# Small products of a doubling scheme, made per 64 tokens in quarters of the PE array

## What is computed

```
a_mat = where(strict, einsum('bhncd,bhnsd->bhncs', kb, k) * gamma, 0.0)
t_mat = a_mat + eye(C)
u = triangular_solve(t_mat, v * beta, lower, unit_diagonal)
w = triangular_solve(t_mat, kb * exp(gc), lower, unit_diagonal)
...
v_new = u_n - w_n @ S
o     = qd @ S + qk_n @ v_new
S     = S * gl + kd^T @ v_new
```

## Time and profile before

| | us |
|---|---|
| median of 3 runs (lowest to highest) | 4056.29 (4054.85 to 4060.84) |
| the profiled execution | 4052.51 |
| its span, first to last instruction | 4050.7 |
| mean granted TensorE clock | 0.993 of 2.4 GHz |
| the stage with the delta rule and the attention | 428.7 to 923.6, 494.9 long |
| PE busy in the span | 3928.2 |

### The profile page before, as it was taken

One profiled execution on the slowest core, in us unless ns is written; L12 is line 12 of the kernel. 1 busy time (PEld: TensorE's weight loads), 2 busy tenths in 40 slices (PEclk: granted clock), 3 DMA queues, 4 the chain that ended last, 5 costly groups with the idle time before them and its releaser, 6 DMA issues.

```text
span 4050.7 us, 47347 instructions
## 1 busy us (share of the span) xinstructions
PE 3928.2 (97%) x19500; PEld 3204.4 (79%) x19500; DVE 2166.8 (53%) x3208; ACT 1673.7 (41%) x2626; POOL 17.1 (0%) x34
## 2 busy tenths in 40 slices
PE   4999999998999999999999999999999999999999
PEld 2777899886788877887778878987778777778887
DVE  6541555554733465874657846345646446646333
ACT  3351556664433353444534335233335233334333
POOL 0000000000000000000000000000000000000000
PEclk9999999998999999999999999999999999999999
DMA  4112000003242222222222222222222222223232
GB/s 167 53 57 70 10 5 6 23 16 119 83 120 94 94 89 87 75 88 89 89 89 76 82 93 91 87 89 78 83 84 94 89 89 78 80 87 114 94 95 87
DMA packets 113869, 323.44 MB, mean 80 GB/s; under 512 B 26920, under 2 KB 34040, under 8 KB 113656
## 3 DMA queue, kind: packets, MB, share of 16 engines
q1 hardware_dynamic: 111416, 314.91, 24.3%
q0 software_dynamic: 2240, 5.51, 0.7%
HBM read 303.86 MB, written 18.06 MB: 79 GB/s over the span
## 4 chain that ended last, share of the span: by engine, by line
PE 92%; DVE 4%; ACT 2%; DMA 1%; issue 1%; SPq 0%; DVEq 0%; ACTq 0%
PE ps L311 49%; PE ps L289 25%; PE ps L1027 4%; PE ps L1022 2%; PE ps L1316 1%; PE ps L1033 1%; PE ps L1293 1%; PE ps L725 1%; PE ps L2412 1%; PE ps L1301 1%; PE ps L1852 1%; PE ps L421 1%; DVE a L508 0%; PE ps L1103 0%; PE ps L1341 0%
## 5 line engine op out<-in xcount | busy, mean ns | idle before, releaser
L311 PE MATMUL ps<-a,w_hi 128*128 128x512 f32 (+1 forms) x6128 | 1875.2, 391 | 14.9 <-DVE a L508 6.7
L311 PEld LDWEIGHTS ps<-a,w_hi 128*128 128x128 f32 x6128 | 1126.3, 189 | 287.3 <-issue 27.5
L311 PE MATMUL ps<-a,w_lo 128*128 128x512 f32 (+1 forms) x3064 | 1163.4, 386 | 0.0
L262 DVE TENSOR_TENSOR w_lo<-w_raw,w_hi 128x1024 fp32r<-128x1024 f32 x539 | 658.1, 1221 | 447.1 <-ACT w_hi L257 444.1
L257 ACT ACTIVATE w_hi<-w_raw 128x1024 fp32r<-128x1024 f32 x539 | 564.1, 1051 | 564.4 <-DMA w_raw<-in_w_mlp 346.5
L311 PEld LDWEIGHTS ps<-a,w_lo 128*128 128x128 f32 x3064 | 571.3, 189 | 122.9
L289 PE MATMUL ps<-h_hi,w_hi 128*128 128x512 f32 x1536 | 490.0, 401 | 1.9 <-DVE xT L361 1.9
L289 PE MATMUL ps<-h_hi,w_lo 128*128 128x512 f32 x1536 | 481.6, 395 | 0.0
L289 PE MATMUL ps<-h_lo,w_hi 128*128 128x512 f32 x1536 | 481.5, 395 | 0.0
L356 DVE TENSOR_TENSOR h_lo<-u_sq,h_hi 128x512 fp32r<-128x512 f32 x192 | 132.9, 692 | 491.3 <-ACT h_hi L346 491.3
L361 DVE TENSOR_TENSOR xT<-xT,ps 128x1024 f32<-128x1024 f32 x192 | 234.1, 1220 | 289.9 <-PE ps L289 289.1
(11 more groups left out here) (358 smaller groups left out, 3328.4 us busy)
## 6 DMA issues: line engine op xcount, KB each, us to landing
w_raw<-in_w_mlp SPq DMA_DIRECT2D x384, 512.0 KB, 3.4
w_raw<-in_w_in SPq DMA_DIRECT2D x107, 512.0 KB, 3.5
w_raw<-in_w_out SPq DMA_DIRECT2D x48, 512.0 KB, 3.5
xT<-in_x SPq DMA_DIRECT2D x2, 2048.0 KB, 11.6
x<-xT SPq DMA_DIRECT2D x2, 2048.0 KB, 7.6
xT<-x SPq DMA_DIRECT2D x2, 2048.0 KB, 12.7
rpb_rows<-in_rpb SPq DMA_DIRECT2D x1, 3810.0 KB
z<-staged SPq DMA_DIRECT2D x4, 512.0 KB, 3.8
```

Of the source, the lines that this page charges most:

```text
L262: nc.vector.tensor_tensor(w_lo[u.z][:, :], w_raw[u.z][:, :], w_hi[u.z][:, :].bitcast(F32), ALU.subtract).then_inc(w_split[u.z], 1)
L311: last = nc.tensor.matmul(ps[:, bank, 0:t1 - t0], w[:, k * P:(k + 1) * P], a[:, h, low, k, t0:t1], start=(i_k == 0 and i == 0), stop=(i_k ...
```

## The change

Up to level 5 each product of `half_heads` becomes two: tokens 0 to 63 with tokens 0 to 63, and 64 to 127 with 64 to 127. Each takes 64 rows and 64 columns of the array (a quarter of it, the two on its diagonal) and 32 moving columns in place of 64, and writes to 64 partitions of the same bank. The blocks off the diagonal are no longer written; the mask of the level is 0 there, and DVE's L1208 reads the bank in whole as before. The subtraction (L1215) is made for the two quarters apart, so that it reads only what was written; the semaphore is raised by the second. Level 6 is as it was.

```diff
+        def quarters(l):
+            if l == NL - 1:
+                return [(slice(0, P), slice(0, 1))]
+            n = GRID >> l + 1
+            return [(slice(GRID * i, GRID * i + GRID), slice(n * i, n * i + n)) for i in range(2)]
...
             def half_heads(b, lhsT, rhs, l, which):
                 for h in range(GH):
-                    last = nc.tensor.matmul(halves(pbank(b), l, which)[:, h], lhsT[:, h, :], halves(rhs[:, :, :], l, which)[:, h],
-                                            start=True, stop=True)
+                    for side, pairs in quarters(l):
+                        last = nc.tensor.matmul(halves(pbank(b), l, which)[side, h, pairs], lhsT[side, h, side],
+                                                halves(rhs[:, :, :], l, which)[side, h, pairs], start=True, stop=True)
                 return last
...
                         dve.wait_ge(gs["X"], upper(n, d, l))
                         dve.wait_ge(gs["Dt"], level(n, d, l - 1))
-                        part = halves(g_Dt[d][:, :, :], l, 1 - d)
-                        nc.vector.tensor_tensor(part, part, halves(pbank(cross_bank(d, l)), l, 1 - d), ALU.subtract).then_inc(gs["Dt"], 1)
+                        for side, pairs in quarters(l):
+                            part = halves(g_Dt[d][:, :, :], l, 1 - d)[side, :, pairs]
+                            ins = nc.vector.tensor_tensor(part, part, halves(pbank(cross_bank(d, l)), l, 1 - d)[side, :, pairs], ALU.subtract)
+                        ins.then_inc(gs["Dt"], 1)
```

## The result

The changed kernel takes 4028.16 us (median of 6 runs, 4025.7 to 4030.75), the kernel before beside it 4056.26 (4054.85 to 4061.45). The ratio is 0.9928, 95% interval 0.9917 to 0.9939: 28 us less, where 29 were forecast. The profiled execution took 4026.77 us with a span of 4025.0, 25.7 less than before.

A forecast was written before the change was run, and what follows sets the result against it. PE's order of work was taken to bound the stage; 80 blocks saving 39.2 us, less 3.7 and 5.9 held back by ACT, gave -29.6 us, 4027 us as median. The range was 4007 to 4079, the forecast's own 4007 to 4038.

The forecast's parts named there:

- The bound: Stage of the edited function, 428.7 to 923.6 us: PE never runs dry and its order of work sets the length.
- A couple's price: Two quarter records, one per row half, in a changed block: 0.062 us a couple, 16 couples 0.99 us.
- The estimate of 0.100 a couple: Changed blocks: if a 25 ns start-to-start floor held for loads too, 0.100 us a couple, +10 us, 4066.
- do two row groups run together?: Changed blocks on PE: yes, from L2412's 64-row operands; a couple costs what one full-array record costs, 0.111 us.
- The change of form: PE going between full array and quarters: 0.30 us for entering and leaving a block, ends 0.25 and 0.40.
- What ACT doesn't let through: PE's L1301 waiting for ACT's copies: 0.73 us lost in each of 5 chunks, 3.7 us.
- The last three chunks: PE already waits for ACT there: the saving of four blocks a chunk counted as lost, 5.9 us.
- One of the prediction's low cases: Changed blocks at 0.062 us, form changes 0.40, same ACT loss: 0.39 a block, 31 - 8 = 23 us, 4033.
- Same bank: Rival: both quarters write one PSUM bank and run one behind the other, +40 us, 4096; chance 0.12.
- Issue: Rival: PE's instruction stream sets the pace, so a couple stays at 0.111 us, +24 us, 4080; chance 0.13.
- Gain eaten: Rival: PE waits at g_D, g_gu or g_Dt, or couples take 0.070 to 0.086; at most half stays, 4038 to 4048; chance 0.12.
- DVE's split: Subtraction L1215 in two: 15 us more of DVE, covered by PE's other work, costing nothing; uncovered, at most 8 us.

The follow-up runs named there:

- e3: Changed kernel, but each product takes all 128 rows and 64 columns of the array, still 32 moving columns: 4025.2 us, ratio 0.9912.
- e2: Changed kernel, but quarters for direction 0 only, in products and subtraction, direction 1 as before: 4053.0 us, ratio 0.9985.
- e6: Changed kernel with the first two of the attention's four copies a row made by DVE in place of ACT: 4019.7 us, ratio 0.9903.
- e8: Kernel before, with every product of levels 1 to 6 made in two column halves, all 128 rows and 64 moving columns, one subtraction: 4018.8 us, ratio 0.9902.
- e10: The changed kernel measured once more, nothing altered: 4025.2 us, ratio 0.9911.
- e9: Kernel before, with all products of levels 1 to 6 in column halves and two attention copies a row on DVE: 4008.9 us, ratio 0.9866.
- e1: Changed kernel, but all four heads of tokens 0 to 63 come ahead of those of tokens 64 to 127: 4049.0 us, ratio 0.9976.
- e7: Changed kernel, but levels 1 to 4 in four pieces of 32 tokens, with four subtractions in place of two: 4026.5 us, ratio 0.9921.
- e4b: Changed kernel with each of DVE's two subtractions made in two again, two heads each: 4030.9 us, ratio 0.9930.

## Why the prediction was right

**The bound.** PE's order of work set the stage's length, as the earlier trace rows had been read: up to chunk 4 what the blocks save comes off the chunk but for one new wait.

**A couple's price** was mis-sized by little: 0.062 us forecast, 0.058 measured. Its way there was right (loads set the pace, columns count, rows don't). The estimate of 0.100 a couple, named there among the rivals, is out with it. But "do two row groups run together?" was the question for the wrong dimension: e3 shows that the rows are not needed.

**The change of form:** 0.30 forecast, 0.34 by e2 and e6. A block saves 0.54 us (e6's early chunks, 5.40/10), where 0.49 were in the sum: 43 us for 80 blocks in place of 39.

**What ACT doesn't let through** in chunks 0 to 4 was 3.7 us in the sum. The first quarter product starts at 430.1 us and its chunk ends 45.4 later; before it was 428.9 and 49.7, so chunk 0 saved 4.3. With chunks 1 to 4 of the table that is 22.2 of 5 x 5.4 = 27.0: 4.8 us lost. e6 shows the cause, for the 0.95 us a chunk come back when the two copies leave ACT.

**The last three chunks** were the step that was mis-sized: 5.9 us forecast, 16.2 - 6.1 = 10.1 measured. The prediction counted ACT there and named a fall of the clock only among the things that would make it wrong. PE's waits grew from 4.5 us to 11.3. The clock is the rest: before, one window of the three was below 1.00 (0.97 of 65.3 us); in the changed kernel 0.97 of 65.4 and 0.92 of 64.7 us. The second of these stands against e8, whose last chunk has the same waits (2.1 us n_pt, 1.4 g_D, 1.1 g_vt, as here) and no fall:

```profile
825.90:885.50 59.60, 54.30 (x695) 47.72 (x694) 32.47 (x98) 45.83 (x98) 0.00 (x0) 1.00 0.14 37
```

59.6 us against 64.7. Some 0.8 us of the 5.1 belong to the level 6 that e8 shortens (57.82 - 57.05 = 0.77 in early chunks), about 4 to the clock; half of 10.2 us at half speed is 5.1. Other traces agree. The table adds up, by the granted clock of each trace, how long it stood at 0.50 while PE had work; the last chunk mark is the product with g_R that ends the chunk table above:

| | last three chunks, us | of it at 0.50 | last chunk mark to the end, us | of it at 0.50 | that less half of the column before |
|---|---|---|---|---|---|
| before | 196.5 | 3.4 | 3126.3 | 34.1 | 3109.3 |
| changed | 190.4 | 13.7 | 3127.7 | 37.5 | 3108.9 |
| e10, changed again | 192.8 | 20.5 | 3124.4 | 30.7 | 3109.1 |
| e3 | 188.6 | 10.2 | 3127.8 | 37.5 | 3109.0 |
| e6 | 182.9 | 10.2 | 3132.3 | 47.8 | 3108.4 |
| e8 | 182.6 | 3.4 | 3129.1 | 41.0 | 3108.6 |
| e9 | 177.2 | 3.4 | 3134.8 | 47.8 | 3110.9 |

e3's chunks are as long as the changed kernel's where both have the full clock. Between e3 and e10 the last three differ by 4.2 us for 10.3 us more at 0.50. The changed kernel has 10.3 us more at 0.50 than the kernel before, so an estimate from these rows is that 4.2 of the 10.1 us are the clock's, and 5.9 are left for ACT, which is what the prediction had counted for it. So what failed in this term is that it had nothing for the clock. What decides when the clock falls no run shows: waits of PE aren't needed for it (e1).

These two errors, +4 us on the blocks and -5 on what is held back, cancel. The stage is 28.3 us shorter; 1.2 were lost ahead of it (its first product comes at 430.1 in place of 428.9) and 1.4 behind it, so the two profiled executions are 25.7 apart, where the sum had 29.6. That the sum met the time so closely is luck, and so is the median that it met, since the second measurement gave 36 us; that it lay within the range is not. One of the prediction's low cases is mis-added: it speaks of the same loss to ACT and takes 8 us where the sum has 9.6, which would make it 4035 in place of 4033.

**The rivals.** *Same bank* is out: 32 loads in 1.01 us, two row groups into one bank. The Trainium skill, TensorEngine Tiling (Array Packing), Gotcha 1: PSUM Pressure, says that different row tiles can't access a bank simultaneously; with different partitions in that bank, the 1.01 us disagree, and the measurement decides. Whether it holds for the same partitions no run tried. *Issue* is out: e7 sends out 64 loads and 64 matmuls in about 0.65 us. *Gain eaten* took a third of it, 15 of 43 us, less than the half that I had given that case.

**DVE's split** cost nothing, as forecast, and e4b doubled it for nothing.

**After the stage** 1.4 us of the 27.1 by which the last chunk mark comes earlier are given back. Of e6's 12.9 us against the changed kernel at that mark its span shows 8.3, of e9's 23.2 it shows 16.1. The table's last columns say where these go. The work behind the mark is the same in all, and what differs is how long the clock stood at 0.50: less half of that time, it is 3108.4 to 3109.3 us in six of the seven. e9's 2 us more are one wait, for n_z, of 13.0 us in place of 10.8. Why those later falls come where they do is open.

## What to carry to other kernels

Where a small product is bound by its weight loads, split its output in halves of the array's columns and issue the halves in turn: loads of half the width then run side by side, with nothing left out of the product and no rows to give up. Keep such products together, since entering and leaving them costs about 0.34 us, and alternate the parts. Then look at what the freed PE runs into: here another engine's copies, and a clock that fell more often among the short blocks, with PE waiting between them (the changed kernel, e7) and without (e1), while e8 and e9 had no more of it in the stage than the kernel before. Where the clock's share differs between two traces, compare chunks that had the full clock.

## What the runs showed of the hardware

- Four parts of 32 rows and columns run together: the first four loads and four matmuls start within 0.03 us from 545.56 (e7):

```profile
L1037 PEld LDWEIGHTS ps<-g_Dt,g_A x4: 101/101/101, 545.6 to 545.6; 32*32 32x32 f32 x4
L1037 PE MATMUL ps<-g_Dt,g_A x4: 198/198/198, 545.6 to 545.6; 32*32 32x16 f32 x4
```

- PE starts records of another quarter past ones that wait for theirs, but only some (e1: 1.32 us a block, between 1.01 alternating and the 1.86 that one by one would be).
- With the products cut into quarters or smaller, the clock fell to 0.50 in places where it had stood at 1.00. Before the fall PE had been busy for 3.56 of 6.20 us (changed), 1.95 of 3.40 us (e7) and 3.40 of 3.40 us (e1).
- What a stretch at 0.50 costs where PE sets the pace is close to half its length: from the last chunk mark to the end, e6 takes 7.8 us more than e10 with 17.1 us more at 0.50.
